# A depthwise convolution of 31 taps: who makes its eight tiles, where the accumulators lie, and in which stage the taps stand

## What is computed

```
ca, cb = jnp.split(cglu, 2, axis=-1)
c = ca * jax.nn.sigmoid(cb)
c = causal_dwconv(c, conv_dw[i]) + conv_dw_bias[i]     # 31 taps, each channel by itself
c = jax.nn.silu(layernorm(c, conv_ln_gain[i], conv_ln_bias[i]))
y_b = c @ w_conv_out[i]
```

## Time and profile before

| | us |
|---|---|
| median of three executions | 1250.44 |
| lowest, highest | 1247.12, 1254.53 |
| span of the profiled execution | 1247.2 |
| busy: TensorE, VectorE, ScalarE, GpSimd | 1151.7, 914.8, 565.1, 315.3 |

### The profile page before, as it was taken

One profiled execution on the slowest core, in us unless ns is written; L12 is line 12 of the kernel. 1 busy time (PEld: TensorE's weight loads), 2 busy tenths in 40 slices (PEclk: granted clock), 3 DMA queues, 4 the chain that ended last, 5 costly groups with the idle time before them and its releaser, 6 DMA issues.

```text
span 1247.2 us, 25963 instructions
## 1 busy us (share of the span) xinstructions
PE 1151.7 (92%) x9340; PEld 1133.4 (91%) x9340; DVE 914.8 (73%) x1321; ACT 565.1 (45%) x791; POOL 315.3 (25%) x349
## 2 busy tenths in 40 slices
PE   5987589999998999999979768999999989999996
PEld 4977589999998999999979758999999989999996
DVE  6599999898766555455779999988976655545566
ACT  5332455434744544343653334644365444434443
POOL 0199960001102000001218999000030020000012
PEclk9999889999999999999999898999999999999999
DMA  5733323445555355445334333344445534554540
GB/s 215 274 136 123 133 101 121 168 168 176 182 192 193 125 189 202 167 171 203 136 138 170 102 136 136 105 168 163 175 158 200 193 135 174 198 203 156 188 163 34
DMA packets 29232, 201.70 MB, mean 162 GB/s; under 512 B 3504, under 2 KB 3696, under 8 KB 5568
## 3 DMA queue, kind: packets, MB, share of 16 engines
q1 hardware_dynamic: 27504, 195.38, 44.3%
q0 software_dynamic: 1088, 4.74, 1.1%
q10 hardware_dynamic: 528, 0.15, 0.0%
HBM read 199.18 MB, written 3.69 MB: 163 GB/s over the span
## 4 chain that ended last, share of the span: by engine, by line
PE 70%; DVE 11%; issue 10%; DMA 3%; ACT 3%; DVEq 1%; ACTq 0%; SPq 0%
PE bank L296 21%; PE bank L298 21%; PE bank L297 21%; DVE w_lo L774 4%; DVE cacc L881 3%; DMA w_raw<-in_wstream 3%; PE bank L331 1%; PE bank L332 1%; PE bank L334 1%; ACT w_hi L509 1%; DMA idt<-in_ident 1%; PE bank L399 1%; DVE rstd L783 1%; DVE zacc L961 1%; DVEq L879 1%
## 5 line engine op out<-in xcount | busy, mean ns | idle before, releaser
L296 PE MATMUL bank<-h_hi,w_hi 128*128 128x256 f32 x1856 | 536.3, 289 | 24.2 <-DVE w_lo L774 17.6
L297 PE MATMUL bank<-h_lo,w_hi 128*128 128x256 f32 x1856 | 529.3, 285 | 0.0
L298 PE MATMUL bank<-h_hi,w_lo 128*128 128x256 f32 x1856 | 529.1, 285 | 0.0
L774 DVE TENSOR_TENSOR w_lo<-w_raw,w_hi 128x2048 fp32r<-128x2048 f32 x183 | 429.6, 2350 | 69.6 <-ACT w_hi L509 69.3
L509 ACT ACTIVATE w_hi<-w_raw 128x2048 fp32r<-128x2048 f32 (+1 forms) x185 | 351.2, 1901 | 228.7 <-DMA w_raw<-in_wstream 186.4
L296 PEld LDWEIGHTS bank<-h_hi,w_hi 128*128 128x128 f32 x1856 | 360.8, 194 | 32.3 <-DVE w_lo L774 20.3
L297 PEld LDWEIGHTS bank<-h_lo,w_hi 128*128 128x128 f32 x1856 | 360.8, 194 | 0.1
L298 PEld LDWEIGHTS bank<-h_hi,w_lo 128*128 128x128 f32 x1856 | 360.3, 194 | 0.0
L296 PE MATMUL bank<-act_hi,w_hi 128*128 128x256 f32 x896 | 253.9, 283 | 0.0
L297 PE MATMUL bank<-act_lo,w_hi 128*128 128x256 f32 x896 | 253.6, 283 | 0.0
L298 PE MATMUL bank<-act_hi,w_lo 128*128 128x256 f32 x896 | 253.5, 283 | 0.0
(11 more groups left out here) (132 smaller groups left out, 956.5 us busy)
## 6 DMA issues: line engine op xcount, KB each, us to landing
w_raw<-in_wstream SPq DMA_DIRECT2D x184, 1024.0 KB, 4.8
rel_bias_rows<-rel_bias_by_distance POOLq DMA_DIRECT2D x1, 2560.0 KB, 17.9
bias<-rel_bias_rows POOLq DMA_DIRECT2D x1, 1536.0 KB, 13.6
xs<-in_x SPq DMA_DIRECT2D x2, 512.0 KB, 4.6
out_y<-xs SPq DMA_DIRECT2D x4, 256.0 KB, 2.0
zacc<-in_p POOLq DMA_DIRECT2D x2, 256.0 KB, 4.2
prms<-in_prm SPq DMA_DIRECT2D x1, 320.0 KB, 10.1
idt<-in_ident ACTq DMA_DIRECT2D x1, 64.0 KB, 8.0
```

Of the source, the lines that this page charges most:

```text
L296: nc.tensor.matmul(o, wh, hi, start=first, stop=False, skip_group_check=True)
L297: nc.tensor.matmul(o, wh, lo, start=False, stop=False, skip_group_check=True)
L298: return nc.tensor.matmul(o, wl, hi, start=False, stop=last, skip_group_check=True)
L774: nc.vector.tensor_tensor(w_lo[:, n % RING, :], w_raw[:, n % RAW_RING, :], f32(w_hi[:, n % RING, :]), ALU.subtract).then_inc(lo_ready, 1)
```

## The change

GpSimd makes no tile any more; it only adds tiles up. VectorE makes all eight, which are 248 taps a layer where it made 186. The accumulators move to PSUM: tiles 0, 1 and then 4, 5 share bank 5, tiles 2, 3 and then 6, 7 share bank 7. Since attention needs these banks, tiles 0 to 3 have to be done ahead of the attention stage, and TensorE waits for that (one added wait). Tiles 4 to 7 are made after it. The order of the first 124 taps comes from a small planner, `_tap_order`: at each place it takes the tile with the fewest taps done. There are 9 taps in a step of `cglu`, 11 in one of `qkv` (8 in the fifth, none in the sixth), none in `sc`, 12 in each of `attn_out` and 14 in each of the first two of `sc_out`.

```diff
+EARLY_CONV = (0, 1, 2, 3)
+LATE_CONV = (4, 5, 6, 7)
+CGLU_TAPS, QKV_TAPS, ATTN_TAPS, SC_TAPS = 9, 11, 12, 14
...
+    for chunk in range(DT + (2 * KT + QT) // 2):
+        for _ in range(CGLU_TAPS if chunk < DT else QKV_TAPS):
+            left = [t for t in EARLY_CONV if t <= chunk and done[t] < CONV_WIDTH]
+            if left:
+                t = min(left, key=lambda u: done[u] if u != (order[-1][0] if order else None) else done[u] + .5)
+                order.append((t, done[t]))
+                done[t] += 1
...
+    return in_cglu, order + [(t, k) for k in range(CONV_WIDTH) for t in LATE_CONV]
...
-        cacc = sb("cacc", [P, 3, SEQ])
+        cacc = [psum[5 + t % 4 // 2 * 2][:, t % 2 * SEQ:(t % 2 + 1) * SEQ] for t in range(DT)]
...
                 v_transpose()
+                pe.wait_ge(conv_step, L * len(DVE_TAPS) + EARLY_TAPS)
...
-                            ins = nc.vector.scalar_tensor_tensor(out=o, in0=src, scalar=w, in1=cacc[:, e, :],
+                            ins = nc.vector.scalar_tensor_tensor(out=o, in0=src, scalar=w, in1=cacc[t],
...
-                    taps(TAPS[0] if t >= 2 else 0)
+                    taps(min(CGLU_TAPS * (t + 1), CGLU_DONE))
                 for j in range((2 * KT + QT) // 2):
-                    taps(TAPS[1])
+                    taps(min(CGLU_DONE + QKV_TAPS * (j + 1), EARLY_TAPS))
...
-                                if k < SC_WIDTH - 1:
-                                    taps(TAPS[2])
...
-                    taps(TAPS[3][j % SC_WIDTH])
...
-                    taps(TAPS[4])
+                    taps(EARLY_TAPS + ATTN_TAPS * (j + 1))
...
-                        taps(TAPS[5] if j < MEAN_AT - 2 else len(DVE_TAPS))
+                        taps(EARLY_TAPS + ATTN_TAPS * DT + SC_TAPS * (j + 1) if j < MEAN_AT - 2 else len(DVE_TAPS))
...
-                pool.wait_ge(pool_prm, L + 1)
...
-                                nc.gpsimd.tensor_scalar(ptmp[:, e, :], cv[:, t, k:k + SEQ], pool_w[:, c:c + 1], 0.0,
-                                                        ALU.mult, ALU.add).then_inc(pool_step, 1)
...
+                for n, t in enumerate(EARLY_CONV[1:] + LATE_CONV):
+                    if n == 0:
+                        pool.wait_ge(conv_step, L * len(DVE_TAPS) + EARLY_TAPS)
+                    if t == LATE_CONV[0]:
+                        pool.wait_ge(conv_step, (L + 1) * len(DVE_TAPS))
```

More of the change, by code:

```diff
@@ L80, with _tap_order @@
 KEYS = P + CHUNK
[L82 to L87, removed]
+EARLY_CONV = (0, 1, 2, 3)
+LATE_CONV = (4, 5, 6, 7)
+CGLU_TAPS, QKV_TAPS, ATTN_TAPS, SC_TAPS = 9, 11, 12, 14
+def _tap_order():
+    order, done = [], [0] * DT
+    for chunk in range(DT + (2 * KT + QT) // 2):
[5 more added lines that the diff above has]
+                done[t] += 1
+        if chunk == DT - 1:
+            in_cglu = len(order)
+    assert all(done[t] == CONV_WIDTH for t in EARLY_CONV)
+    return in_cglu, order + [(t, k) for k in range(CONV_WIDTH) for t in LATE_CONV]
+CGLU_DONE, DVE_TAPS = _tap_order()
+EARLY_TAPS = CONV_WIDTH * len(EARLY_CONV)
 MEAN_AT, VAR_AT = 3, 6
@@ L861, in tap_count, with taps @@
                 def tap_count(t, k):
[L863 to L868, removed]
+                    return L * len(DVE_TAPS) + DVE_TAPS.index((t, k)) + 1
+                def taps(upto):
+                    for a in range(at[0], upto):
+                        t, k = DVE_TAPS[a]
                         w = prms[:, L, CONV_W + t * CONV_WIDTH + k:CONV_W + t * CONV_WIDTH + k + 1]
@@ L872, in taps @@
                             wait_read(dve, L, 2 * t + 1, (2 * t + 1) % BANKS)
[L873 to L876, removed]
+                            ins = nc.vector.tensor_scalar(cacc[t], src, w, prms[:, L, CONV_B + t:CONV_B + t + 1],
                                                           ALU.mult, ALU.add)
@@ L1146, in _ @@
             with pool.Fori(0, DEPTH) as L:
-                pool.wait_ge(pool_prm, L + 1)
[L1149 to L1164, removed]
-                                nc.gpsimd.tensor_scalar(ptmp[:, e, :], cv[:, t, k:k + SEQ], pool_w[:, c:c + 1], 0.0,
-                                                        ALU.mult, ALU.add).then_inc(pool_step, 1)
[L1167 to L1170, removed]
-                            o = pacc[:, e, :] if k < CONV_WIDTH - 1 else cv[:, t, CPAD:]
-                            nc.gpsimd.tensor_tensor(o, pacc[:, e, :], ptmp[:, e, :], ALU.add).then_inc(pool_step, 1)
-                            n += 1
-                            made[e] = n
-                        summed = [max(m, g) for m, g in zip(made, summed)]
@@ L1176, in _ @@
-                pool.wait_ge(pool_step, L * POOL_STEPS + n)
-                for t in range(1, DT):
-                    for n, tiles in enumerate(DVE_ROUNDS):
-                        if t == max(tiles[0], 1):
-                            pool.wait_ge(conv_step, L * len(DVE_TAPS) + CONV_WIDTH * sum(map(len, DVE_ROUNDS[:n + 1])))
-                    if t > 1:
-                        pool.wait_ge(csum_step, L * 2 * (DT - 1) + t - 1)
-                    a = cv[:, 0, CPAD:] if t == 1 else sqsum[:, :]
+                for n, t in enumerate(EARLY_CONV[1:] + LATE_CONV):
[3 more added lines that the diff above has]
+                        pool.wait_ge(conv_step, (L + 1) * len(DVE_TAPS))
+                    if n:
+                        pool.wait_ge(csum_step, L * 2 * (DT - 1) + n)
+                    a = sqsum[:, :] if n else cv[:, EARLY_CONV[0], CPAD:]
```

13 lines of the change are left out of this document (2 added, 11 removed).

## The result

The changed kernel takes 1265.5 us (median of four executions, 1264.34 to 1267.75) against 1249.24 for the kernel before (four, 1247.12 to 1254.53): a ratio of 1.0123, 95% interval 1.0096 to 1.015. It is slower, by 16 us; the forecast was 1265. The profiled execution has a span of 1263.2 us where before it was 1247.2.

What follows compares the result with a forecast made beforehand. TensorE, busy 1151.7 of 1247.2 us, was taken to set the end except where it waits for VectorE. Gains of 36.3 and losses of 50.8 us gave 1261.7 for the profiled execution, median 1265, range 1235 to 1290.

Steps and rivals of the forecast that it cites:

- clock behind the mean's pause: TensorE behind the new pause before the mean: the lowered clock costs 2.0 us a layer.
- The price of a tap in PSUM: VectorE tap reading and writing PSUM: taken as 0.397 us, between a lower bound of 0.34 and a mirrored 0.46.
- A: Rival: a tap in PSUM is cheaper, 0.34 us, and the kernel gets faster, 1237 us; chance 0.25.
- B: Rival: a tap in PSUM is dearer, 0.46 us, 31 us more, 1296 us; chance 0.17.
- The dependent tap: VectorE tap directly following its own tile's previous tap: 0.63 us, so a run of nine takes 5.3 us.
- Ahead of attention: Stages before attention: TensorE waits for VectorE's 124 early taps; pair 1 starts 9.5 us (first layer) and 6.3 us (second) earlier.
- The attention stage: Pair 1 to pair 5: VectorE's work falls below TensorE's 8.86 us a step; gains 12.1 and 8.4 us.
- Rival D: First layer: chunk loads or a wait keep TensorE back, half of 21.6 us goes, 1276 us; 0.46 together with the forecast.
- Up to the mean: From `attn_out` to the mean: 124 late taps and four GpSimd additions take 80.7 us instead of 57.3, 23.4 later.
- Rival C: Small terms are cheap, 0.51 us a dependent tap and 3.4 us for the four additions: 1254 us; chance 0.12.

Runs made afterwards that it cites:

- e1: Changed kernel with the accumulators of the eight tiles in SBUF instead of PSUM, order of taps unchanged: 1264.66 us, ratio 1.0128 to the kernel before.
- e6: Changed kernel with tiles 6 and 7 left unconvolved, 62 late taps left out, 7 taps a step instead of 12: 1215.8 us.
- e7: Changed kernel with the mean and the variance each taken one chunk of sc_out later: 1268.5 us, ratio 1.0136 to the kernel before.
- m1: Mixture of both kernels: GpSimd makes tiles 2 and 3, VectorE 0, 1, 4, 5 before attention and 6, 7 after, accumulators in PSUM: 1216.91 us.
- m2: The same mixture as m1 with VectorE's accumulators in SBUF instead of PSUM: 1270.85 us, ratio 1.0171 to the kernel before.
- m1b: m1 run once more, unchanged, on the same chip as its variant: 1215.74 us, ratio 0.9724 to the kernel before.
- m3: m1 with VectorE making only 0, 1, 4 before attention; 5, 6, 7 accumulate in SBUF, spread from the attention stage on: 1225.34 us.
- e3: Kernel before without GpSimd's taps, tiles 2 and 3 left unconvolved, VectorE's work unchanged: 1187.24 us, ratio 0.9486.

## Why the prediction was right, point by point

| term | forecast, us | measured, us |
|---|---|---|
| entry to attention (pair 1), first and second layer | -9.5, -6.3 | -8.0, -5.7 |
| pair 1 to pair 5 | -12.1, -8.4 | -11.8, -8.1 |
| first gate product of `attn_out` to mean, a layer | +23.4 | +23.0 |
| clock behind the mean's pause, first and second layer | +2.0, +2.0 | +2.1, +2.0 |
| span | +14.5 | +16.0 |

The measured values: 137.46 - 129.44 = 8.0; in the second layer from the first gate product (650.31 before, 655.32 after) to pair 1, 97.8 and 92.1. Pair 1 to pair 5 was 47.0 and 43.3 us and is 35.2 in both (164.63 - 129.44 and 782.65 - 747.46). To the mean 80.3 after 57.3. Mean to variance in the first layer 19.8 (322.62 - 302.82) after 17.7 (317.40 - 299.70), in the second 19.7 after 17.7, for the clock. By these terms -33.6 + 50.1 = 16.5, where the spans give 16.0. The median lies 2.3 us above the profiled span, where 3.2 were taken. The span came out 1.5 us above the forecast and this difference 0.9 below, so that the median is met within 1 us is in part luck.

- **The price of a tap in PSUM.** 0.397 taken, 0.39 measured, and 480 against 481 ns in e1. It was a choice among three prices, and most of the chance that the forecast left to another outcome (rivals A and B) hung on it; it is e1 that settles it. The argument held that the earlier trace rows show no difference between an input from a bank and one from SBUF. With that A and B fall. The rule of the Trainium skill that spoke against the change ("VectorE: DVE Perf Modes", "The TRN2 errata — SBUF-src ops pay a fixed extra latency per instruction"), by which a PSUM source would cost an estimated 65 ns more, is not seen in these rows: it would have added an estimated 32 us, and the sum came out within 2.
- **The dependent tap.** 0.63 taken and measured: eight from 680.90 to 685.74, 7 x 0.63 + 0.40 = 4.8. What the step missed is the first tap: the next starts 0.68 us after it, where 0.35 + 0.15 had been taken. So a run is 5.5 instead of 5.3 us, and four of them are 0.7 us.
- **Ahead of attention.** In the second layer pair 0 starts at 739.28; the last early tap had been forecast for 733.3, which is 738.3 here, since the layer begins 5.0 us later (655.32 for 650.31). So it is 1.0 us late, 0.7 of it for the four first taps. From there to pair 1 it was 8.2 for 8.5. In the first layer pair 0 starts at 119.89 for 119.4, and pair 1 9.55 us later for 8.5: here the clock behind the pause cost 3.2 us (last section) and not the 2.0 taken. The term that was mis-sized by most is thus the clock behind a short pause: what hangs on it came out 1.05 us too long one time and 0.3 too short the other.
- **The attention stage.** The step "VectorE's work is below TensorE's 8.86 us" held: 35.2 us without a gap, and no waits between the pairs. Rival D falls, since the first layer gained 19.8 of the forecast 21.6.
- **Up to the mean.** The sum 58.2 + 17.1 + 5.2 + 0.16 gave 80.7, and it was 80.3: last tap at 75.1 (75.3), four additions 4.95 (5.2). Some ahead-running of TensorE was lost in three small waits, 1.2 us at most each; one wait of 18.6 took nearly all, as told, released by GpSimd. e6 shows the cause by taking it away, and e7 shows that it is not the place of the mean.
- **Rival C** (cheap small terms) falls with the 0.63; the four additions took 4.95 us, near the 5.2 and not the 3.4.

## What to carry to other kernels

Ask of each engine's stages where TensorE already waits for it and where it has slack, and price a move of work by the stage that it lands in: 62 more taps in a stage in which VectorE had 5 us to spare (52.05 of 57.30 busy) cost 23 us, and the same kernel gained 12 and 8 where VectorE had been the bound. An accumulator in PSUM cost a tap nothing here (481 ns against 480), and took it out of the contention with GpSimd; that helps only where GpSimd works beside it (54 us between m1 and m2, nothing in e1), so it is a reason to keep GpSimd's share of the work, not to take it away. Moving the point at which TensorE waits shortens that wait but does not bring the mean forward, and what is won in front is given back behind: what sets the time, here the last tap, has to be moved (e7).

## What the runs showed of the hardware that I had not expected

- A VectorE operation with two SBUF inputs can be held up for whole microseconds by GpSimd instructions that follow each other without a gap: a `w_lo` of 2.28 us took 8.21 (m1), 8.73 (m1b) and 9.29 us (m3). In the kernel before, where VectorE's taps contended themselves, GpSimd's were slowed as well: two multiplications and two additions took 1.27 + 1.77 us there, and 0.95 + 1.42 in m1. With the taps in PSUM they don't slow GpSimd, and what of VectorE still needs both inputs from SBUF seems to pay for it. The kernel before and m2 have no `w_lo` over 2.87 us, and m2 differs from m1 in the place of the accumulators alone. That the one causes the other is argued from these rows; I made no run that spaces GpSimd out.
- A first tap (multiply and bias, L879) takes 0.54 us into PSUM, and 0.41 into SBUF in e1; for the taps behind it there is no such difference. Into SBUF it is also not safe from GpSimd, although it has one tensor input only: in e3 the four first taps that ran while GpSimd added tiles took 0.73 to 0.88 us.
- What a pause costs in clock does not follow its length. Behind the pause of 18.6 us 4 us passed at a granted clock of 0.50, behind the 4.3 us in e7 too, and behind the two of 3.2 us at the entry to attention it differs between the layers:

```profile
119.90:123.90 4.00, 4.00 (x20) 3.56 (x21) 2.37 (x2) 2.27 (x2) 3.82 (x3) 0.50 0.51 164
123.90:126.90 3.00, 3.00 (x18) 3.00 (x17) 3.00 (x5) 0.13 (x1) 0.17 (x1) 0.59 0.71 289
...
739.30:741.30 2.00, 2.00 (x16) 1.77 (x17) 2.00 (x1) 0.35 (x1) 1.99 (x1) 0.87 0.51 205
741.30:743.30 2.00, 2.00 (x12) 2.00 (x11) 0.45 (x2) 2.00 (x2) 1.84 (x3) 0.50 0.53 82
743.30:747.40 4.10, 4.10 (x32) 4.03 (x31) 4.07 (x7) 1.06 (x2) 0.15 (x1) 0.89 0.70 248
```

These are stretches of the changed kernel behind the two entries. Each is at 0.50 (1.2 GHz) for a time: 4 x 0.50 + 3 x 0.41 = 3.2 us are lost in the first layer, 2 x 0.13 + 2 x 0.50 + 4.1 x 0.11 = 1.7 in the second, behind waits of the same length. Why the second falls later and less stays open.
